# Four layers of a small transformer on one core: another passage from section to section

## The chip, the cores and the metric

The kernel runs on 1 core of one Trainium2 chip. The metric is the device time of one execution in microseconds (us), the median of several runs. Engines: TensorE (PE, and PEld for its weight loads), VectorE (DVE), ScalarE (ACT), GpSimd (POOL), and SyncE (SP), which issues the loads.

## The reference, cut to what matters

256 tokens of width 2048 pass through two layers with a mixer and an MLP each (`first_block`), and through two hybrid attention layers (`second_block`). Each of the six sections ends in the same way: a product with an output matrix, a norm over the features, an addition to the residual `h`; and the next section begins with a norm of the new `h`.

```python
def rmsnorm(x, g):
    y = x * lax.rsqrt(jnp.mean(x * x, axis=-1, keepdims=True) + RMS_EPS)
    return y * g

# first_block, per layer
mix = mixer(rmsnorm(h, norm_mix_pre[layer]), ...)          # ends in "@ w_out" or "@ w_o"
h = h + rmsnorm(mix, norm_mix_post[layer])
f = jnp.square(jax.nn.relu(rmsnorm(h, norm_mlp_pre[layer]) @ w_up)) @ w_down
h = h + rmsnorm(f, norm_mlp_post[layer])
# second_block, per layer
out = y @ w_out
x = x + rms_norm(out, post_w)
```

All of it is float32.

## The kernel before

**Layout.** Features lie on the partitions, tokens along the free axis: `h` is 16 blocks of 128 features x 256 tokens. All weight matrices are laid into one stream of chunks of 128 x 2048 values (1 MB). One chunk is one product: 16 units of 128 x 128, accumulated into one PSUM bank `acc[s]`, s = chunk number modulo 4.

**Float32 products from rounded parts.** Each chunk is split: ScalarE writes the rounded `w_high` (L719), VectorE the rest `w_low = raw - w_high` (L1119). Activations are split likewise (`x[:, kt, 0]` high, `x[:, kt, 1]` low). `high_unit` (L285) multiplies `w_high` with both activation parts side by side, 512 columns: the left half of the bank gets high x high, the right half high x low. `low_unit` (L292) adds `w_low` x high activations to the right half, 256 columns. Then ScalarE copies the right half to `corr` (L729), and VectorE adds the left half and `corr` (`sum_halves`, L1128). Both engines work three chunks ahead (`ahead`). The four `raw` buffers are loaded by SyncE, each load waiting for the product that used the buffer four chunks earlier (L251, L267 to L273).

**The passage.** In the output sections each block goes to `branch[b]`; after an MLP, VectorE adds it to the `branch[b]` of the earlier quarters (L1238). ScalarE squares the block (L735) and multiplies it by the norm's gain (`gain`, L754). GpSimd adds up the squares of blocks 0 to 14 (`add_squares`, L1077). After the last product `stat_post` on TensorE sums GpSimd's sum and the last square over the features (columns of ones, L354). VectorE's `mean` (L1139) divides, GpSimd's `root` (L1083) takes the power -0.5, VectorE writes two diagonal matrices from it (L1143), and TensorE multiplies them with ones (`spread`, L362), so that every partition of the bank `extra` has the scale of each token. `norm` on VectorE then goes through groups of one or two blocks (`NORM_GROUPS`): `step = branch * scale` (L1170), `h += step` (L1175), and `xs_low` (L1154), the low part of the next section's input; ScalarE writes the high part (L738) and the square of the new `h` (L735), and GpSimd adds these squares.

**The order.** Every engine's order is written out by hand, with counting semaphores between the engines; loops are hardware loops (`Fori`). TensorE starts the next section with `product_first`: chunks c, c+1 and c+2 together, block by block as `xs` becomes ready. Product c+3 follows, and has in its unit 0 (`STAT_AT`) the feature sums of the next norm and in unit 8 (`SPREAD_AT`) its spread. VectorE, in `norm`, does the subtraction of chunk c+2 between `mean` and the first step, that of c+3 behind the last `xs_low`, and then the mean and the copy of the scale to `scale_pre` (`norm_scale`, L1149), which the first results of the section need. There are five such passages, the sixth norm (c is None) is followed by the output's DMAs only. The two last layers are one loop of two turns, whose body on VectorE begins with `norm`'s part of the previous section and ends with `out_section`.

**Names used below.** r counts the norms' roots (24 in all), m the norms behind a section (0 to 5), n the norms ahead of one. PSUM banks `score[0]` and `score[1]` belong to the attention heads.

## Time and profile before

| | |
|---|---|
| median of 3 runs | 3194.34 us (3192.07 to 3197.99) |
| profiled execution: span, first to last instruction | 3191.0 us |
| instructions | 50316 |
| TensorE busy | 3054.0 us, 96% of the span |
| VectorE busy | 2115.3 us, 66% |
| ScalarE busy | 1591.5 us, 50% |
| GpSimd busy | 270.1 us, 8% |
| mean granted TensorE clock | 0.984 of full speed |
| DMA | 548.23 MB, mean 172 GB/s |

The profile is of one execution; its own time is the span and what lies around it (start and end of the program), and the runs' median is the number to compare. A row of a timeline has the start in us from the span's beginning, the duration in us, the engine, the line, the operation, `output<-inputs`, shapes, the count of merged instructions, and in brackets the idle time ahead of it and what ended it. Durations overlap slightly where instructions follow one another directly. A fp32 matmul appears as two records.

### The profile page before, as it was taken

The numbers are of one execution on the slowest core, as the hardware profiler recorded it, in microseconds if no ns is written. First come the engines' busy times: TensorE is split into PE (matmuls) and PEld (weight loads), VectorE is DVE, ScalarE is ACT, GpSimd is POOL, SyncE is SP. The second block draws the span as 40 slices with busy tenths as digits, with TensorE's granted clock in tenths as the row PEclk, the third lists the DMA queues.
The fourth block names the chain that finished last, engine by engine and source line by source line (L and its number), as shares of the span: only waits on it lengthen the run. The fifth ranks groups of instructions, "written<-read, shape, count | busy, mean of one in ns | idle before, by whom it ended". The sixth has DMA issues, their size and how long they took to land.

```text
span 3191.0 us, 50316 instructions
## 1 busy us (share of the span) xinstructions
PE 3054.0 (96%) x17552; PEld 2660.9 (83%) x17552; DVE 2115.3 (66%) x2969; ACT 1591.5 (50%) x2364; POOL 270.1 (8%) x206
## 2 busy tenths in 40 slices
PE   7999899999999899999999999999899998899997
PEld 6888788888888788887888888887788877788876
DVE  4776765756566677765756666665878655878655
ACT  5445544434444565555434444445657454657454
POOL 1002300000001300003000000003100003100003
PEclk9999999999999999999999999999999999999998
DMA  5555455555555344444555555554344434444434
GB/s 204 184 184 189 151 188 185 193 187 186 192 187 185 135 176 167 169 169 145 193 189 186 192 188 185 193 188 171 134 170 147 157 136 156 146 168 149 146 140 164
DMA packets 76413, 548.23 MB, mean 172 GB/s; under 512 B 8464, under 2 KB 8976, under 8 KB 10384
## 3 DMA queue, kind: packets, MB, share of 16 engines
q1 hardware_dynamic: 76304, 546.81, 47.7%
q8 instruction: 64, 1.05, 0.1%
q14 instruction: 45, 0.37, 0.0%
HBM read 544.68 MB, written 2.10 MB: 171 GB/s over the span
## 4 chain that ended last, share of the span: by engine, by line
PE 34%; issue 12%; POOL 3%; DVE 3%; ACT 1%; DMA 0%; POOLq 0%; DVEq 0%; ACTq 0%; SPq 0%
PE acc L285 20%; PE acc L292 10%; POOL sum_sq L1077 3%; PE acc L667 1%; PE score L385 1%; DVE w_low L1119 1%; DVE h L1175 0%; PE acc L674 0%; ACT w_high L719 0%; DVE step L1170 0%; PE head_out L412 0%; ACT swapped L818 0%; POOL small L1083 0%; PE score L393 0%; POOL sum_sq L1072 0%
## 5 line engine op out<-in xcount | busy, mean ns | idle before, releaser
L1119 DVE TENSOR_TENSOR w_low<-raw,w_high 128x2048 fp32r<-128x2048 f32 x514 | 1175.9, 2288 | 343.4 <-ACT w_high L719 343.0
L285 PE MATMUL acc<-xs,w_high 128*128 128x512 f32 x4962 | 1268.9, 400 | 50.3 <-DVE xs L1154 31.8
L285 PEld LDWEIGHTS acc<-xs,w_high 128*128 128x128 f32 x4962 | 921.2, 191 | 258.2 <-DVE xs L1154 39.0
L719 ACT ACTIVATE w_high<-raw 128x2048 fp32r<-128x2048 f32 x515 | 979.9, 1903 | 29.8 <-DMA raw<-stream 28.9
L729 ACT ACTIVATE corr<-acc 128x256 f32<-128x256 f32 x512 | 195.5, 382 | 1230.8 <-PE acc L292 1201.0
L285 PE MATMUL acc<-inner,w_high 128*128 128x512 f32 x3072 | 736.3, 391 | 2.8 <-DVE inner L1192 2.8
L292 PE MATMUL acc<-xs,w_low 128*128 128x256 f32 x4962 | 689.3, 285 | 0.9 <-DVE w_low L1119 0.9
L292 PEld LDWEIGHTS acc<-xs,w_low 128*128 128x128 f32 x4962 | 661.5, 194 | 25.1 <-DVE w_low L1119 1.4
L285 PEld LDWEIGHTS acc<-inner,w_high 128*128 128x128 f32 x3072 | 564.0, 188 | 112.6 <-DVE inner L1192 3.7
L1128 DVE TENSOR_TENSOR y<-acc,corr 128x256 f32<-128x256 f32 x408 | 172.3, 422 | 398.5 <-ACT corr L729 397.1
L292 PEld LDWEIGHTS acc<-inner,w_low 128*128 128x128 f32 x3072 | 393.7, 191 | 15.1
L292 PE MATMUL acc<-inner,w_low 128*128 128x256 f32 x3072 | 398.3, 283 | 0.0
L1077 POOL TENSOR_TENSOR sum_sq<-sum_sq,sq 128x256 f32<-128x256 f32 x162 | 230.3, 1421 | 285.7 <-ACT sq L735 278.8
L1072 POOL TENSOR_TENSOR sum_sq<-sq 128x256 f32<-128x256 f32 x12 | 21.0, 1754 | 1978.5 <-ACT sq L735 1960.8
L1128 DVE TENSOR_TENSOR branch<-acc,corr 128x256 f32 (+1 forms) x96 | 40.5, 422 | 121.4 <-ACT corr L729 121.4
L818 ACT ACTIVATE swapped<-y 32x256 f32<-32x256 f32 (+1 forms) x208 | 86.5, 416 | 42.0 <-DVE y L1128 39.1
L825 ACT ACTIVATE prob<-prob,small 128x128 f32<-128x128 f32 (+1 forms) x144 | 64.5, 449 | 70.7 <-DVE small L1276 41.3
L775 ACT ACTIVATE inner<-source 128x256 f32 (+1 forms) x176 | 71.7, 407 | 54.8 <-DVE source L1516 24.3
L1134 DVE TENSOR_TENSOR scaled<-y,scale_pre 128x256 f32<-128x256 f32 x208 | 88.4, 425 | 10.9
L738 ACT ACTIVATE xs<-h,col 128x256 fp32r<-128x256 f32 x96 | 46.8, 500 | 65.5 <-DVE h L1175 65.5
L1192 DVE TENSOR_TENSOR inner<-source,inner 128x256 f32 (+1 forms) x176 | 73.6, 418 | 1.9 <-ACT inner L775 1.9
L1083 POOL TENSOR_TENSOR small<-small,minus_half 128x2 f32<-128x2 f32 x24 | 16.7, 695 | 586.7 <-DVE small L1139 586.7
(141 smaller groups left out, 1339.1 us busy)
## 6 DMA issues: line engine op xcount, KB each, us to landing
raw<-stream SPq DMA_DIRECT2D x515, 1024.0 KB, 4.8
h<-x_t SPq DMA_DIRECT2D x4, 512.0 KB, 7.9
out<-h SPq DMA_DIRECT2D x4, 512.0 KB, 2.6
consts<-tables SPq DMA_DIRECT2D x1, 960.0 KB, 16.5
branch<-w_spatial SPq DMA_DIRECT2D x1, 512.0 KB, 17.3
branch<-b_spatial SPq DMA_DIRECT2D x1, 512.0 KB, 18.1
prob_t<-lambdas SPq DMA_DIRECT2D x1, 256.0 KB, 18.2
col<-columns SPq DMA_DIRECT2D x1, 136.0 KB, 2.1
```

The source lines that it names most:

```text
L285: nc.tensor.matmul(acc[s][:, :], w_high[:, s, kt * P:(kt + 1) * P], x[:, kt, :, :], start=(kt == first_of[0]), stop=False, skip_group_chec ...
L292: return nc.tensor.matmul(acc[s][:, TOKENS:], w_low[:, s, kt * P:(kt + 1) * P], x[:, kt, 0, :], start=False, stop=stop, skip_group_check=True)
L719: nc.scalar.activation(w_high[:, s, 0:units * P], raw[:, s, 0:units * P], ACT.Copy)\
L729: nc.scalar.activation(corr[:, s % 2, :], acc[s][:, TOKENS:], ACT.Copy).then_inc(corr_ready, 1)
L775: nc.scalar.activation(dyn2(inner, b, 0), source[:, s, :], ACT.Copy).then_inc(sem("inner_high"), 1)
L818: cp = nc.scalar.activation(swapped[a:a + half, :], src[b:b + half, :], ACT.Copy)
L825: nc.scalar.activation(prob[:, bank, lo:hi], prob[:, bank, lo:hi], ACT.Exp, bias=neg_max(bank, t), accum_out=denom(bank, t)).then_inc(sem( ...
L1077: nc.gpsimd.tensor_tensor(sum_sq[:, :], sum_sq[:, :], sq[:, b % 2, :], ALU.add)\
L1119: V.tensor_tensor(w_low[:, s, 0:units * P], raw[:, s, 0:units * P], w_high[:, s, 0:units * P], ALU.subtract).then_inc(low_ready, 1)
L1128: V.tensor_tensor(y[:, s % 2, :] if to is None else to, acc[s][:, 0:TOKENS], corr[:, s % 2, :], ALU.add)\
L1134: V.tensor_tensor(to, y[:, s % 2, :], scale, ALU.mult).then_inc(sem(done), 1)
L1192: V.tensor_tensor(dyn2(inner, b, 1), source[:, s, :], dyn2(inner, b, 0), ALU.subtract)\
```

## The change

1. The last product of the three output sections and of the two MLPs' last quarters (`product_last`, `last_products`) accumulates all three partial products into the left half of the bank: 32 matmuls of 256 columns with `w_high`, 16 with `w_low`. Between the two parts TensorE waits for GpSimd's fifteenth square sum and does its column sums. For this block `corr_out` and `sum_halves` go; ScalarE squares it from PSUM and writes `branch` with the gain in one activation (behind an MLP VectorE first adds it to `branch`). Small instructions keep the counters `corr_ready` and `summed` in step (`corr_skipped` on ScalarE, a copy of two columns to `unused` on VectorE).
2. `spread` has no diagonal: the root, broadcast along 128 columns, is the stationary operand and the identity the moving one, once for each half of the tokens. The two diagonal instructions and the buffer `diag` go, for all 24 roots.
3. In `norm` the product `branch * scale` is written to the PSUM banks `score[0]` and `score[1]` in turn instead of to `step`, and `h` is added from there; the wait of each multiply for the previous addition goes.
4. The subtraction (and the rounding) of chunk c+2 is done at the end of the output section, ahead of the mean, by the ordinary `ahead`.
5. `STAT_AT` goes from 0 to 4, `SPREAD_AT` from 8 to 12. `product_first` waits for one sum less. The sines and exponentials that ScalarE computed ahead of the first MLP come behind its first quarter. The last four blocks of the sections, and the last MLP quarter on TensorE, are written out behind the loops.

```diff
-STAT_AT, SPREAD_AT = 0, 8
+STAT_AT, SPREAD_AT = 4, 12
...
+            def product_last(c, s, x, m):
+                whole = acc[s][:, 0:TOKENS]
+                pe.wait_ge(high_ready, c + 1)
+                pe.wait_ge(summed, c - 3)
+                for kt in range(KB):
+                    for part in range(2):
+                        nc.tensor.matmul(whole, w_high[:, s, kt * P:(kt + 1) * P], x[:, kt, part, :],
+                                         start=(kt == 0 and part == 0), stop=False)
+                pe.wait_ge(sem("square_added"), squares_post(m) + KB - 1)
+                column_sums(sum_sq[:, :], True, False)
+                pe.wait_ge(low_ready, c + 1)
+                for kt in range(KB):
+                    mm = nc.tensor.matmul(whole, w_low[:, s, kt * P:(kt + 1) * P], x[:, kt, 0, :],
+                                          start=False, stop=(kt == KB - 1))
+                mm.then_inc(product_done, 1)
...
-                pe.wait_ge(summed, at(c))          # product_first
+                pe.wait_ge(summed, c - 1)
...
             def spread(r):
-                pe.wait_ge(sem("diag_ready"), r + 1)
-                nc.tensor.matmul(extra[:, 0:TOKENS], ones, diag[:, :], start=True, stop=True)\
-                    .then_inc(sem("spread_done"), 1)
+                pe.wait_ge(sem("root_ready"), r + 1)
+                for n in range(TB):
+                    mm = nc.tensor.matmul(extra[:, n * P:(n + 1) * P], root_of[:, n:n + 1].to_broadcast([P, P]), ident,
+                                          start=True, stop=True, skip_group_check=True)
+                mm.then_inc(sem("spread_done"), 1)
             def stat_post(m, r):
-                pe.wait_ge(sem("square_added"), squares_post(m) + KB - 1)
                 pe.wait_ge(sem("squared"), squares_post(m) + KB)
-                sum_over_features([sum_sq[:, :], sq[:, 1, :]], "square_added")
+                column_sums(sq[:, 1, :], False, True).then_inc(sem("square_added"), 1)
                 spread(r)
...
+            def corr_skipped(c):                   # ScalarE
+                act.wait_ge(summed, c - 1)
+                nc.scalar.activation(corr[:, 1, 0:TB], acc[3][:, 0:TB], ACT.Copy).then_inc(corr_ready, 1)
...
+                def last(b, s):                    # ScalarE, out_section
+                    ahead(c0 + b, s)
+                    square(acc[s][:, 0:TOKENS], squares_post(m) + b, s,
+                           lambda: act.wait_ge(product_done, c0 + b + 1))
+                    nc.scalar.activation(branch[:, b, :], acc[s][:, 0:TOKENS], ACT.Copy,
+                                         scale=column(G_POST + KB * m + b)).then_inc(sem("gained"), 1)
+                    corr_skipped(c0 + b)
...
             def root(r):                           # GpSimd
                 pool.wait_ge(sem("mean_ready"), r + 1)
+                pool.wait_ge(sem("spread_done"), at(r))
...
             def mean(r, count, eps, stat_sem, value):
                 dve.wait_ge(sem(stat_sem), value)
+                dve.wait_ge(sem("root_ready"), at(r))
                 V.tensor_scalar(mean_of, extra[:, TOKENS:TOKENS + TB], 1.0 / count, eps, ALU.mult, ALU.add)\
                     .then_inc(sem("mean_ready"), 1)
-                dve.wait_ge(sem("root_ready"), r + 1)
-                for n in range(TB):
-                    op = V.tensor_scalar(diag[:, n * P:(n + 1) * P], ident, root_of[:, n:n + 1], None, ALU.mult)
-                op.then_inc(sem("diag_ready"), 1)
...
                 mean(r, D, NORM_EPS, "square_added", squares_post(m) + KB)     # norm
-                if c is not None:
-                    low(c + 2, 2)
...
+                    stepped = score[i % 2][:, 0:width * TOKENS].rearrange("p (a t) -> p a t", a=width)
                     dve.wait_ge(sem("gained"), KB * m + b + width)
-                    dve.wait_ge(sem("h_ready"), at(KB * m + b))
-                    V.tensor_tensor(step[:, 0:width, :], branch[:, b:b + width, :], scale, ALU.mult)\
+                    V.tensor_tensor(stepped, branch[:, b:b + width, :], scale, ALU.mult)\
                         .then_inc(sem("step_ready"), width)
...
-                    V.tensor_tensor(h[:, b:b + width, :], h[:, b:b + width, :], step[:, 0:width, :], ALU.add)\
+                    V.tensor_tensor(h[:, b:b + width, :], h[:, b:b + width, :], stepped, ALU.add)\
                         .then_inc(sem("h_ready"), width)
...
+                if c is not None:
+                    dve.wait_ge(summed, c - 1)
+                    dve.wait_ge(corr_ready, c)
+                    V.tensor_copy(unused, acc[3][:, 0:TB]).then_inc(summed, 1)
                 for i in late:
                     xs_low(n, i)
...
+                        c = c0 + 2 * KB * q + 2 * KB - 1                      # VectorE, last MLP quarter
+                        ahead(c, 3)
+                        dve.wait_ge(product_done, c + 1)
+                        V.tensor_tensor(branch[:, KB - 1, :], branch[:, KB - 1, :], acc[3][:, 0:TOKENS], ALU.add)\
+                            .then_inc(sem("down_added"), 1)
```

## Rows read from the trace of the kernel before

**Rows 1.** The page: busy times, and the costliest ScalarE group (busy, mean ns).
```profile
PE 3054.0 (96%) x17552; PEld 2660.9 (83%) x17552; DVE 2115.3 (66%) x2969; ACT 1591.5 (50%) x2364; POOL 270.1 (8%) x206
...
L719 ACT ACTIVATE w_high<-raw 128x2048 fp32r<-128x2048 f32 x515 | 979.9, 1903 | 29.8 <-DMA raw<-stream 28.9
```

**Rows 2.** Timeline of PE, first passage: start, us, engine, line, operation, [idle before].
```profile
347.80 2.07 PE L292 MATMUL acc<-inner,w_low 128*128 128x256 f32 x16
...
351.89 0.59 PE L354 MATMUL extra<-consts,sq 128*128 128x1 f32 x4
354.02 1.22 PE L362 MATMUL extra<-diag,consts 128*128 128x256 f32 x2 [1.55 <-DVE diag L1143]
358.16 0.77 PE L285 MATMUL acc<-xs,w_high 128*128 128x512 f32 x1 [2.92 <-DVE xs L1154]
```

**Rows 3.** Timeline of VectorE, first passage.
```profile
352.51 0.16 DVE L1139 TENSOR_SCALAR small<-extra 128x2 f32<-128x2 f32 x1 [1.76 <-PE extra L354]
353.48 0.48 DVE L1143 TENSOR_SCALAR diag<-consts,small 128x128 f32<-128x128 f32 x2 [0.81 <-POOL small L1083]
353.88 2.28 DVE L1119 TENSOR_TENSOR w_low<-raw,w_high 128x2048 fp32r<-128x2048 f32 x1
356.08 0.41 DVE L1170 TENSOR_TENSOR step<-branch,extra 128x256 f32<-128x256 f32 x1
```

**Rows 4.** Windows, first passage: width, PE PEld DVE ACT POOL busy, clock, DMA.
```profile
354.00:356.00 2.00, 1.22 (x2) 0.50 (x2) 2.00 (x1) 0.00 (x0) 0.00 (x0) 0.50 0.06 25
358.16:381.74 23.58, 21.52 (x97) 16.75 (x97) 22.37 (x31) 15.24 (x35) 11.92 (x15) 0.88 0.00 1
```

**Rows 5.** Chain of waits: a product of 32 matmuls of 256 columns.
```profile
3031.17 3.84 PE acc L667 x32
```

**Rows 6.** Timeline of GpSimd, end of the last product.
```profile
346.91 2.54 POOL L1077 TENSOR_TENSOR sum_sq<-sum_sq,sq 128x256 f32<-128x256 f32 x1 [3.02 <-ACT sq L735]
```

**Rows 7.** Timeline of SyncE, and the page's row of the weight loads.
```profile
344.49 0.33 SPq L251 DMA_DIRECT2D raw<-stream  x1
...
raw<-stream SPq DMA_DIRECT2D x515, 1024.0 KB, 4.8
```

**Rows 8.** Timeline of VectorE, fifth passage, behind a jump back.
```profile
2698.69 0.16 DVE L1139 TENSOR_SCALAR small<-extra 128x2 f32<-128x2 f32 x1 [6.25 <-issue]
```

**Rows 9.** Timeline of VectorE, second passage, behind an MLP.
```profile
1082.88 0.16 DVE L1139 TENSOR_SCALAR small<-extra 128x2 f32<-128x2 f32 x1 [1.76 <-PE extra L354]
```

**Rows 10.** Timeline of VectorE inside the norm step, first passage.
```profile
359.48 1.22 DVE L1175 TENSOR_TENSOR h<-h,step 128x512 f32<-128x512 f32 x1
...
369.56 0.68 DVE L1170 TENSOR_TENSOR step<-branch,extra 128x512 f32<-128x512 f32 x1
370.16 1.03 DVE L1154 SCALAR_TENSOR_TENSOR xs<-h,col,xs 128x256 fp32r<-128x256 f32 x1
...
376.83 1.23 DVE L1175 TENSOR_TENSOR h<-h,step 128x512 f32<-128x512 f32 x1
```

**Rows 11.** Timeline of VectorE, the last norm step.
```profile
3177.59 0.69 DVE L1175 TENSOR_TENSOR h<-h,step 128x512 f32<-128x512 f32 x1
3178.41 0.69 DVE L1170 TENSOR_TENSOR step<-branch,extra 128x512 f32<-128x512 f32 x1
```

**Rows 12.** Timeline of GpSimd inside the norm step, first passage.
```profile
359.33 0.82 POOL L1072 TENSOR_TENSOR sum_sq<-sq 128x256 f32<-128x256 f32 x1 [5.88 <-issue]
```

**Rows 13.** Timeline of PE, end of the first three products and after.
```profile
381.74 0.50 PE L354 MATMUL extra<-consts,sum_sq 128*128 128x1 f32 x4
...
389.37 1.88 PE L285 MATMUL acc<-xs,w_high 128*128 128x512 f32 x7 [0.74 <-ACT w_high L719]
```

**Rows 14.** Timeline of VectorE, end of the norm step and the scale.
```profile
379.93 2.82 DVE L1119 TENSOR_TENSOR w_low<-raw,w_high 128x2048 fp32r<-128x2048 f32 x1
...
384.91 0.42 DVE L1149 COPY scale_pre<-extra 128x256 f32<-128x256 f32 x1 [0.79 <-PE extra L362]
```

**Rows 15.** Timeline of PE, a head's spread in the third layer.
```profile
2370.46 0.91 PE L362 MATMUL extra<-diag,consts 128*128 128x256 f32 x2 [2.54 <-DVE diag L1143]
```

More of the change, by code:

```diff
@@ L416, in weigh, with last_products, out_section, mlp_section @@
                 mm.then_inc(sem("head_done"), 1)
-            def out_section(c0, split0, late, order=None, hooks=None):
+            def last_products(c, m):
+                for s in range(3):
+                    product(c + s, s, inner)
+                product_last(c + 3, 3, inner, m)
+            def out_section(c0, split0, late, m, order=None, hooks=None):
                 product_early(c0, split0, late, order, hooks)
                 product(c0 + 3, 3, inner)
-                with pe.Fori(1, KB // 4) as i:
+                with pe.Fori(1, KB // 4 - 1) as i:
                     for s in range(4):
                         product(c0 + 4 * i + s, s, inner)
-            def mlp_section(c0, split0, n, r):
-                def quarter(q, first):
+                last_products(c0 + KB - 4, m)
+            def mlp_section(c0, split0, n, r, m):
+                def quarter(q, first, last):
                     c = c0 + 2 * KB * q
@@ L436, in quarter @@
                     product(c + 3, 3, inner)
-                    with pe.Fori(1, KB // 4) as i:
+                    with pe.Fori(1, KB // 4 - int(last)) as i:
                         for s in range(4):
                             product(c + 4 * i + s, s, inner)
-                quarter(0, True)
-                with pe.Fori(1, FFN_QUARTERS) as q:
-                    quarter(q, False)
+                    if last:
+                        last_products(c + KB - 4, m)
+                quarter(0, True, False)
+                with pe.Fori(1, FFN_QUARTERS - 1) as q:
+                    quarter(q, False, False)
+                quarter(FFN_QUARTERS - 1, False, True)
             product(0, 0, xs, ready=lambda kt: pe.wait_ge(sem("xs_ready"), kt + 1))
@@ L1195, in out_section, with one @@
             def out_section(c0):
-                def four(i, last):
-                    for s in range(4):
-                        c = c0 + 4 * i + s
-                        sum_halves(c, s, dyn(branch, 4 * i + s))
-                        if s < 3 or not last:
-                            ahead(c, s)
-                with dve.Fori(0, KB // 4 - 1) as i:
-                    four(i, False)
-                four(KB // 4 - 1, True)
+                def one(i, s):
+                    c = c0 + 4 * i + s
+                    sum_halves(c, s, dyn(branch, 4 * i + s))
+                    ahead(c, s)
+                with dve.Fori(0, KB // 4 - 1) as i:
+                    for s in range(4):
+                        one(i, s)
+                for s in range(3):
+                    one(KB // 4 - 1, s)
+                ahead(c0 + KB - 1, 3)
             def mlp_section(c0, split0, up0):
```

137 lines of the change are left out of this document (73 added, 64 removed).

## The prediction

> **What bounds the kernel.** I read the page first. TensorE is busy 96% of the span [rows 1], so only a time in which it waits can be won. In the long sections it does not wait; it waits where one section passes to the next. There are six such passages (five lead into three products computed together, the sixth is the last norm step), so I read the first in the timelines engine by engine, and laid the others beside it.
>
> The last product ends at 347.80 + 2.07 = 349.87, the next real matmul starts at 358.16: 8.29 us [rows 2]. The links: the ScalarE copy, the VectorE sum and the square of block 15 lie before the column sums that end at 352.48 [rows 2]; mean at 352.51, 0.81 for GpSimd's root, two diagonals of 0.48, then `w_low` of chunk 18 until 356.16, although the spread ended at 354.02 + 1.22 = 355.24 [rows 2, 3]. The step starts at 356.08, so the mean-to-step distance is 3.57, and 2.08 more pass to the first matmul.
>
> Behind it VectorE paces TensorE. From 358.16 to 381.74 VectorE is busy 22.37 of 23.58 us, TensorE idle 2.06, at a mean clock of 0.88 [rows 4]. That is (1 - 0.88) / 0.5 x 23.58 = 5.7 us at 1.2 GHz, the rest at 2.4; the clock had fallen while TensorE had only sums and the spread [rows 4].
>
> **The gap, behind a mixer (passages 1, 3, 5).** The last product becomes 32 + 16 narrow matmuls. The same form elsewhere takes 3.84 for 32 [rows 5], which is 0.12 each, so the high part lasts about what 16 wide ones last; I add 0.2. Between the parts TensorE now waits for GpSimd's add of block 14, which ends at 346.91 + 2.54 = 349.45, since a VectorE subtraction runs at the same time [rows 6]. So 1.5 us of stall, 0.5 for four column sums (0.59 with the pipeline end [rows 2]) and 2.07 for the low part: the product ends near 352.1, 2.2 later. In return the corr copy and the VectorE sum go, and the square starts at once: 352.1 + 0.45, sums 0.59, mean possible at 353.3.
>
> But the moved subtraction has its own chain. Load issued 344.49, landed 4.8 later [rows 7] at 349.3; `w_high` 1.90 [rows 1] to 351.2; `w_low` 2.28 [rows 3] to 353.5. It stands ahead of the mean on VectorE, so the mean starts at 353.45, 0.94 later than now. Root and spread follow as before, without the diagonals (0.03 + 0.48), and without the 0.85 by which `w_low` outlasted the spread: mean to step 3.57 - 0.51 - 0.80 = 2.26. Step at 355.7: **0.35 earlier**. If the load landed a microsecond later this turns to a loss of 0.65; if GpSimd alone decided, the gain would be 0.5. The new waits queue the square, the gain and the small skip copy behind `w_high` on ScalarE; it would have been done 0.9 before the product ends, so nothing is late by it. For the spread, two 128-column products take the place of one of 256: I take the same 1.22; ends: 0.3 shorter (a spread in the third layer takes 0.91 [rows 15]) and 0.6 longer (four records of sums take 0.59).
>
> Passage 5 has a jump back of the layer loop ahead of the mean: 6.25 us of idle without a releaser [rows 8]. The jump is now reached behind `w_low`'s dispatch, about 0.9 later. Same balance: 0.35 earlier.
>
> **Behind an MLP (passages 2, 4).** Here VectorE must still add the last product to `branch`, and that add stands behind `w_low`. In the first passage `w_low` ends 1.0 behind the old mean; here the old mean of 1082.88 [rows 9] already has that add ahead of it, so `w_low` ends 0.5 behind it, at 1083.4. Add 0.41 [rows 3], hop and square 0.55, hop and sums 0.7: mean at 1085.1, 2.2 later; minus 1.31: step **0.9 later**. Bounds: 0 (load earlier) to 2 later. Sum of the five gaps: 3 x -0.35 + 2 x 0.9 = +0.7 us.
>
> **The norm step.** `h` += `step` on 512 columns takes 1.22 to 1.23 nearly everywhere in the five passages, while the sixth, where GpSimd adds no squares, shows 0.69 [rows 10, 11]. In the passage GpSimd's add started at 359.33 and ended at 360.15; `h` started at 359.48 and ended at 360.70, 0.55 behind it [rows 10, 12]: one waits until the other is through. The multiply, which reads `branch` and PSUM, takes 0.68 beside GpSimd [rows 10]. So two SBUF inputs collide and one does not, and with the step in PSUM `h` has one. I take 0.68 for it. A result written to PSUM by VectorE is in no row; lower bound 0.68, upper bound 1.22, the slowest row of the form; I take 0.68, the row with a PSUM operand.
>
> The Trainium skill (VectorE: DVE Perf Modes, the TRN2 errata) charges a PSUM source 62 cycles more than an SBUF one, about 65 ns. By it 54 adds would cost 3.5 us more. The multiply with its PSUM source at 0.68 beside an SBUF-only add at 0.69 speaks against it [rows 10, 11], and the sum below goes by the rows.
>
> Period of a pair of blocks now: 359.48 to 376.83 is six periods, 2.89 each [rows 10]. New: 0.60 multiply (369.56 to 370.16 [rows 10]) + 0.60 add + two `xs_low` of 0.4 (what other work on 256 columns takes, 0.41 [rows 3]) = 2.0, if nothing collides. But `xs_low` has two SBUF inputs, and GpSimd's two adds (0.82 each [rows 12]) still come in each period; the one that collides takes 1.03 [rows 10]. One of two colliding gives 2.6. Five periods save 5 x 0.4 = 2.0; the first saves 0.5 and its multiply no longer waits for the previous add (0.2 twice); the last add 0.55; back go 0.5 where ScalarE's `w_high` in the middle now makes VectorE wait. VectorE is through 3.0 earlier (bounds: 1.0 at the old period, 4.5 at 2.0).
>
> TensorE's floor: 48 pairs of wide and narrow matmuls at 0.12 x 3 = 0.36 [rows 5] are 17.3, plus half of 5.7 cold: 20.1 against 23.58. It can win 3.5 at most; I take 3.0 with VectorE. Then product 4: it waits 0.74 for `w_high`, which comes behind the scale [rows 13], so the scale decides. Now it stands at 384.91, 3.17 behind the end at 381.74 [rows 13, 14]. The spread moves to unit 12: 12 x 0.24 = 2.9, the sums at unit 4 another 0.36, the spread itself 0.79 (the idle time before the copy [rows 14]): 4.05 behind that end, although its input is ready earlier (the diagonals' 0.5 are gone). So 0.9 go back, and of 3.0 remain **2.1 per passage**, 10.5 in five (bounds 1.5 x 5, where VectorE stays the later and saves 1.0 + 0.5, and 3.5 x 5).
>
> **The tail.** Mean 0.9 later, minus 0.5 for the diagonals: +0.4. The multiply no longer waits for the previous add: now 3178.28 to 3178.41 [rows 11], 0.13, and back-to-back instructions overlap by 0.08 (369.56 + 0.68 against 370.16 [rows 10]): 0.21 x 8 = 1.7. Sum -1.3.
>
> **The rest.** Without the diagonal the spreads of the heads come 0.5 earlier; TensorE waits 2.54 for one, and there is one such in each of two layers [rows 15]. Together -1.0 (0 to -2). The first norm and the latent ones lie beside other work. The sines and exponentials that move behind the first MLP quarter fall where ScalarE, busy 50% of the span [rows 1], is three chunks ahead of TensorE: nothing. Without that cover, its 1.90 for one `w_high` is the size of what a product could wait.
>
> **Sum.** +0.7 - 10.5 - 1.3 - 1.0 = -12.1 us on the profiled span of 3191.0. The median of the runs is 3194.34, 3.3 above that span (launch and end around it, unchanged), so 3182.2; I say 3182.
>
> **Rivals.**
> 1. *TensorE becomes the bound.* `xs_low` hardly collides, the period is 2.0 to 2.2 and each passage wins 3.5; gaps as good as zero: 3194.3 - 17.5 - 2.5 (tail and heads) = 3174. For it: the adds that collided most were `h`. Against: GpSimd's work in the passage stays the same. 15%.
> 2. *The gain is eaten at new seams.* New code is laid straight behind loops; if two more seams pay what the fifth does (6.25 of idle where others have 1.76 [rows 3, 8]: 4.5 each), 9 go back: 3191. The same comes out if collisions move to both `xs_low` and the gaps grow 1 us each. Within 0.2%. 20%.
> 3. *Slower: VectorE from PSUM to PSUM.* If multiply and add each take 1.22, the period is 3.2 before collisions, 3.6 with them, 0.7 above now. Seven pairs at 0.7 are 4 to 5 in each passage, 1.08 more for each of seven pairs less 1.7 are 6 in the tail: 3194 + 20 + 6 = 3220. It turns to a loss once both together cost 0.8 more than I take. For it: no row shows a VectorE result in PSUM. Against: reads of PSUM cost nothing extra here. 8%.
> 4. *Slower by the moved subtraction alone:* the chain load, `w_high`, `w_low`, mean runs 3 us longer in every passage because ScalarE takes it late: +15 against -12: 3197. 4%.
>
> My forecast has 53%. Under 0.2% (6.4 us, about what a measurement of this kernel can tell) counts as the same. Faster: 53 + 15 + a few of rival 2, 71%; same 18%; slower 11%. Range 3168 to 3194: down to rival 1 with all bounds good, up to rival 2's end.
>
> **What would show it.** Right: `h` at 0.68 to 0.70 in the passages; `xs_low` still at times near 1.0; a hole of 1.5 us inside each last product; mean later by 0.9 (mixer) and 2.2 (MLP); first three products done in 20.5 us instead of 23.6; a product 4 that still waits for `w_high`. Wrong: a multiply above 0.75, a period above 2.8, idle time without releaser at new seams, or a mean that is not later.

## The result, and the profile after

The changed kernel takes 3167.93 us (median of 4 runs, 3166.22 to 3171.5) against 3193.2 beside it (3191.23 to 3197.99): ratio 0.9917, 95% interval 0.9904 to 0.9929. It is 25 us faster, twice the 12 predicted, and its median lies just outside the range of 3168 to 3194.

The last product in the first passage, TensorE (start, us, ..., [idle before]), against [rows 2]:

```profile
345.75 4.00 PE L318 MATMUL acc<-inner,w_high 128*128 128x256 f32 x32
351.09 0.61 PE L368 MATMUL extra<-consts,sum_sq 128*128 128x1 f32 x4 [1.34 <-POOL sum_sq L1126]
351.56 2.15 PE L324 MATMUL acc<-inner,w_low 128*128 128x256 f32 x16
354.18 0.61 PE L368 MATMUL extra<-consts,sq 128*128 128x1 f32 x4 [0.47 <-ACT sq L766]
355.97 0.71 PE L379 MATMUL extra<-consts,small 128*128 128x128 f32 x4 [1.18 <-POOL small L1133]
358.81 0.77 PE L284 MATMUL acc<-xs,w_high 128*128 128x512 f32 x1 [2.13 <-DVE xs L1201]
```

VectorE beside it, against [rows 3]:

```profile
352.77 2.29 DVE L1169 TENSOR_TENSOR w_low<-raw,w_high 128x2048 fp32r<-128x2048 f32 x1 [2.32 <-ACT w_high L745]
354.98 0.15 DVE L1190 TENSOR_SCALAR small<-extra 128x2 f32<-128x2 f32 x1
356.72 0.43 DVE L1215 TENSOR_TENSOR score<-branch,extra 128x256 f32<-128x256 f32 x1 [1.58 <-PE extra L379]
```

The hole inside the product is there (1.34 us), and `w_low` ends as the mean starts. Counted from the start of the last product, the mean comes 9.23 later where it came 8.36 later (352.51 - 344.15), and the step follows it by 1.74, where it was 3.57.

VectorE in the norm step, against [rows 10], and GpSimd beside it, against [rows 12]:

```profile
363.62 0.68 DVE L1220 TENSOR_TENSOR h<-h,score 128x512 f32<-128x512 f32 x1
364.21 0.48 DVE L1201 SCALAR_TENSOR_TENSOR xs<-h,col,xs 128x256 fp32r<-128x256 f32 x1
364.61 0.69 DVE L1215 TENSOR_TENSOR score<-branch,extra 128x512 f32<-128x512 f32 x1
365.21 0.48 DVE L1201 SCALAR_TENSOR_TENSOR xs<-h,col,xs 128x256 fp32r<-128x256 f32 x1
365.61 0.68 DVE L1220 TENSOR_TENSOR h<-h,score 128x512 f32<-128x512 f32 x1
...
374.01 1.58 DVE L1201 SCALAR_TENSOR_TENSOR xs<-h,col,xs 128x256 fp32r<-128x256 f32 x2
```
```profile
361.58 6.70 POOL L1126 TENSOR_TENSOR sum_sq<-sum_sq,sq 128x256 f32<-128x256 f32 x7 [0.87 <-ACT sq L766]
...
363.45 0.85 POOL L1126 TENSOR_TENSOR sum_sq<-sum_sq,sq 128x256 f32<-128x256 f32 x1
```

`h` fell from 1.22 to 0.68. Of the 80 `xs_low` of the five passages 72 take 0.47 to 0.50. The other eight, 0.67 to 0.88, are the last one or two of each passage, where no instruction of 512 columns with a PSUM operand lies between one `xs_low` and the next (the row at 374.01 merges two of them, 0.69 and 0.87). In the kernel before 35 of 80 were longer than 0.5.

Two blocks take 1.99. That is the undisturbed period; over the same six periods as in the 2.89 of the kernel before, which hold one wait for ScalarE in either kernel, it is 2.13 ((372.76 - 359.97) / 6). GpSimd's seven additions begin 0.99 apart; the first takes 0.73, the others 0.85. Over the five passages its 75 additions take 0.82 on average, where they took 0.81: the time that VectorE no longer loses is not lost by GpSimd instead.

The first three products, against [rows 4] (width, busy time of PE, PEld, DVE, ACT, POOL, granted clock), and in the second line the low part of the last product of the second passage:

```profile
358.81:377.70 18.89, 18.89 (x96) 16.54 (x97) 17.66 (x32) 13.55 (x32) 12.19 (x15) 0.87 0.00 1
1077.00:1080.00 3.00, 3.00 (x15) 2.74 (x13) 2.12 (x1) 0.85 (x1) 0.00 (x0) 0.50 0.00 0
```

They take 18.89 us, not 23.58, and TensorE is never idle in them. Product 4 and the product behind it, against [rows 13, 14]; the third row is the same place in the third passage:

```profile
380.95 0.61 PE L379 MATMUL extra<-consts,small 128*128 128x128 f32 x4
...
386.05 3.93 PE L284 MATMUL acc<-xs,w_high 128*128 128x512 f32 x16 [1.68 <-ACT w_high L745]
...
1519.81 5.53 PE L284 MATMUL acc<-xs,w_high 128*128 128x512 f32 x16 [2.56 <-ACT w_high L745]
```

The wait for `w_high` grew from 0.74 to 1.68, and where it is 2.56 the sixteen matmuls behind it run partly at 1.2 GHz (5.53 for 3.93).

The mean and the copy of the scale cut the whole span into pieces. That is the account used from here on (profiled executions; us):

| kernel | up to first mean | five times mean to scale | five times scale to next mean | last mean to end | span |
|---|---|---|---|---|---|
| before | 352.5 | 162.7 | 2656.9 | 19.0 | 3191.0 |
| changed | 355.0 | 135.6 | 2662.4 | 16.7 | 3169.7 |
| e1 | 354.1 | 139.0 | 2656.1 | 17.3 | 3166.5 |
| e3 | 354.2 | 138.7 | 2672.0 | 17.0 | 3181.9 |
| e4 | 352.9 | 143.4 | 2641.7 | 16.2 | 3154.2 |
| e5 | 354.5 | 132.1 | 2662.3 | 16.7 | 3165.7 |
| e9 | 353.3 | 138.3 | 2659.9 | 16.7 | 3168.2 |
| e11 | 351.8 | 138.3 | 2642.9 | 16.3 | 3149.2 |
| e14 | 351.6 | 137.3 | 2649.2 | 16.3 | 3154.4 |

The change takes 27.1 out of the passages and 2.2 out of the tail, and puts 8.0 (2.5 + 5.5) on the rest. Of the 8.0, 5.8 lie between the start of the last product and the mean: the mean comes 0.87, 2.07, 0.89 and 2.10 later in the first four passages, 2.33 earlier in the fifth and 2.16 later in the sixth. The fifth mean, and the low part of the sixth last product, which ran mostly at 1.2 GHz (3.26 for 2.15):

```profile
2685.60 0.16 DVE L1190 TENSOR_SCALAR small<-extra 128x2 f32<-128x2 f32 x1 [1.14 <-PE extra L368]
3148.19 3.26 PE L324 MATMUL acc<-inner,w_low 128*128 128x256 f32 x16
```

The other 2.2 lie in the sections. Two cautions go with the table. The profiled execution is not the median one: in the changed kernel and e3 it was 3.6 and 2.6 slower than the median, in e4 and e11 2.9 and 6.9 faster. And before and e1, which have the same instructions up to the first mean, differ by 1.6 there. So much can differ in the first and the third column without a cause in the code.

### The profile page after: what moved, and what is told of

Read it like the earlier page. It is cut to its first block, busy times and chain, and to the rows that moved or that the text cites. A ratio compares the mean times of both kernels' runs of the same rounds, so it can differ in the third digit from the quotient of the medians.

```text
span 3169.7 us, 50419 instructions
## 1 busy us (share of the span) xinstructions
PE 3049.9 (96%) x17696; PEld 2676.1 (84%) x17696; DVE 2078.0 (66%) x2921; ACT 1590.9 (50%) x2364; POOL 304.8 (10%) x206
## 4 chain that ended last, share of the span: by engine, by line
PE 41%; issue 5%; DVE 3%; ACT 2%; POOL 1%; DMA 1%; DVEq 0%; POOLq 0%; ACTq 0%; SPq 0%
PE acc L284 24%; PE acc L291 12%; POOL sum_sq L1126 1%; PE score L402 1%; DMA raw<-stream 1%; PE acc L693 1%; ACT w_high L745 1%; DVE w_low L1169 1%; PE acc L700 0%; ACT swapped L866 0%; DVE prob L1323 0%; DVE small L1327 0%; PE extra L379 0%; PE head_out L429 0%; PE score L410 0%
## 5 line engine op out<-in xcount | busy, mean ns | idle before, releaser
L284 PE MATMUL acc<-inner,w_high 128*128 128x512 f32 x2976 | 713.5, 392 | 2.8 <-DVE inner L1241 2.8
L284 PEld LDWEIGHTS acc<-inner,w_high 128*128 128x128 f32 x2976 | 546.8, 188 | 108.8 <-DVE inner L1241 3.7
L291 PEld LDWEIGHTS acc<-inner,w_low 128*128 128x128 f32 x2976 | 381.5, 191 | 14.5
L291 PE MATMUL acc<-inner,w_low 128*128 128x256 f32 x2976 | 386.0, 283 | 0.0
L1126 POOL TENSOR_TENSOR sum_sq<-sum_sq,sq 128x256 f32<-128x256 f32 x162 | 265.2, 1637 | 228.1 <-ACT sq L766 217.7
L1184 DVE TENSOR_TENSOR scaled<-y,scale_pre 128x256 f32<-128x256 f32 x208 | 88.4, 425 | 10.9
L1133 POOL TENSOR_TENSOR small<-small,minus_half 128x2 f32<-128x2 f32 x24 | 16.7, 695 | 596.0 <-DVE small L1190 596.0
```

Of the source, the lines that this page charges most:

```text
L284: nc.tensor.matmul(acc[s][:, :], w_high[:, s, kt * P:(kt + 1) * P], x[:, kt, :, :], start=(kt == first_of[0]), stop=False, skip_group_chec ...
L291: return nc.tensor.matmul(acc[s][:, TOKENS:], w_low[:, s, kt * P:(kt + 1) * P], x[:, kt, 0, :], start=False, stop=stop, skip_group_check=True)
L1126: nc.gpsimd.tensor_tensor(sum_sq[:, :], sum_sq[:, :], sq[:, b % 2, :], ALU.add)\
L1184: V.tensor_tensor(to, y[:, s % 2, :], scale, ALU.mult).then_inc(sem(done), 1)
```

## The experiments

### Which part brings the gain

**e1**, the kernel before with part 3 alone.
```diff
-dve.wait_ge(sem("h_ready"), at(KB * m + b))
-V.tensor_tensor(step[:, 0:width, :], branch[...], scale, ALU.mult)
+V.tensor_tensor(stepped, branch[...], scale, ALU.mult)    # stepped lies in score[g % 2]
```


> The kernel before, with the norm step in PSUM alone (part 3 of the change). Theory A (slots): the addition to h no longer needs both SBUF inputs, GpSimd's adds fit into the 0.6 us slots between two xs_low, so xs_low stays at 0.48 and a pair of blocks takes 2.0 us instead of 2.9; the scale then comes 4 to 5 us earlier in each of five passages, 1.7 us in the tail: 3193 - 20 to 25, about 3171, or some 8 us more if TensorE's clock falls at product 4. Theory B (my forecast: one of two xs_low collides, period 2.5 to 2.6): 2.7 per passage and 1.7, about 3178. Theory C (the gain comes mainly from other parts): above 3185.

Measured: 3169.45 us (3168.21 to 3171.01), ratio 0.9934 (0.9917 to 0.995). That is theory A's time to 2 us, and its durations:

```profile
364.20 0.48 DVE L1154 SCALAR_TENSOR_TENSOR xs<-h,col,xs 128x256 fp32r<-128x256 f32 x1
364.60 0.68 DVE L1175 TENSOR_TENSOR h<-h,score 128x512 f32<-128x512 f32 x1
```

**e2**, the changed kernel with the step back in SBUF: e1's edit undone.

> The changed kernel with the step in SBUF again (part 3 undone). Theory A: additions at 1.22 us beside GpSimd's adds, period 2.9, each passage 3.5 to 4.5 us longer, the tail 1.7: 3168 + 17 to 24, about 3188. Theory C: under +6, below 3174.

Measured: 3196.72 us (3191.41 to 3198.5), ratio 1.0012 (1.0002 to 1.0021). `h` is back at 1.22:

```profile
364.36 1.22 DVE L1221 TENSOR_TENSOR h<-h,step 128x512 f32<-128x512 f32 x1
```

Parts 1, 2, 4 and 5 together bring nothing. Part 3 is the gain. (Not each of the other parts is worth nothing: e4 and e9 below show that one of them costs what the others bring.)

**e3**, the changed kernel with the diagonals (part 2 undone).

> The changed kernel with the two diagonal instructions and the one wide spread (part 2 undone). Theory: 0.5 us for the diagonals and 0.5 us for the wide spread at the low clock in each of six gaps, 0.5 in each of two heads' waits; the scale of the next section hides the rest behind the hook: +6 to +8 us, about 3175. Rival (diagonals lie beside other work, as I priced them but for the tail): +3, 3171.

Measured: 3181.05 us (3177.32 to 3183.97), 13 above the changed kernel. By the table 3.1 of the profile's 12.2 lie in the passages, where the two diagonal instructions (0.48 together [rows 3]) can account for 2.4; 9.6 lie in the sections, whose instructions are the same but for the diagonals of the heads. The mean granted clock was 0.980, against 0.984.

**e10**, the kernel before with parts 3 and 2.

> The kernel before with part 3 (the product of the norm step in PSUM) and part 2 (no diagonal), and nothing else. Part 3 alone gave 3169.5. Theory A (the diagonals are worth what their instructions last on the path: nothing in a passage, where the subtraction behind them fills the time, 0.5 in the tail, 1 to 2 at the heads): 3166 to 3168. Theory B (they are worth what putting them back cost in the changed kernel, 13 us, most of it where TensorE's shorter idle time keeps the granted clock up): 3157 to 3161.

Measured: 3168.95 us, as e1; theory B's 3157 to 3161 is not seen. But its five executions go from 3163.06 to 3180.94, and their clocks with them, from 0.984 to 0.977: 0.007 of 3170 us is 22, the times differ by 18. One kernel, with nothing changed, is so moved by its clock as far as e3 was moved from the changed kernel. Beside e1 the diagonals are worth nothing that this scatter lets one see. That they are worth a few us, what their instructions last, is not shown; the rest of e3's 13 is no property of part 2 that these runs show, though e3's five clocks (0.980 to 0.983) all lie at or below the changed kernel's lowest (0.983).

### Who waited for whom

**e7**, the kernel before, GpSimd adding 2 of 256 columns (sums of the next norm left out but for two tokens).
```diff
-nc.gpsimd.tensor_tensor(sum_sq[:, :], sum_sq[:, :], sq[:, b % 2, :], ALU.add)
+nc.gpsimd.tensor_tensor(sum_sq[:, 0:2], sum_sq[:, 0:2], sq[:, b % 2, 0:2], ALU.add)
```


> The kernel before, with GpSimd's additions of squares ahead of a norm on 2 of 256 columns (leaves out the sum of squares of all tokens but two in five norms; the work of all other engines is the same). Theory A (all that the passage paid in the kernel before is that VectorE and GpSimd wait for one another at SBUF): the additions to h fall to 0.69, xs_low to 0.48, the period of a pair from 2.9 to 2.1 us, product_first from 23.6 to about 19.5, and the kernel to 3170 to 3175. Theory B (the step in SBUF is itself slower, also without GpSimd): h stays at 1.22 in the passages and the time within 5 us of 3193.

Measured: 3173.6 us (3172.19 to 3174.63), ratio 0.9939 (0.9923 to 0.9955). VectorE:

```profile
362.90 0.67 DVE L1171 TENSOR_TENSOR step<-branch,extra 128x512 f32<-128x512 f32 x1
363.50 0.48 DVE L1155 SCALAR_TENSOR_TENSOR xs<-h,col,xs 128x256 fp32r<-128x256 f32 x1
363.91 0.68 DVE L1176 TENSOR_TENSOR h<-h,step 128x512 f32<-128x512 f32 x1
```

With the step in SBUF, but GpSimd nearly quiet, `h` is 0.68 and the period 2.0. Theory A: the 1.22 was GpSimd's doing. The Trainium skill (GPSIMD Engine Reference, Specifications) says that GpSimd contends for SBUF with VectorE instructions that have two SBUF inputs; the runs agree, 1.22 against 0.68, and give it its size.

**e8**, the same cut in the changed kernel.

> The changed kernel with the same cut of GpSimd's additions to 2 columns (leaves out the same sums). Theory A (with the step in PSUM nothing is left of the contention on the path): the period stays at 2.0, xs_low at 0.48, 3165 to 3169; only what GpSimd's last additions delay the sums may be won. Theory B (GpSimd still slows VectorE by half of what it did): the period falls below 1.9 us and the kernel to 3160 or less.

Measured: 3167.17 us (3165.19 to 3169.02), 0.8 below the changed kernel. On VectorE only the eight long `xs_low` at the ends of the passages became shorter (none is above 0.50), and mean to scale takes 135.6 in five passages, as in the changed kernel. Theory A: nothing of the contention is left to win.

**e6**, the changed kernel with sixteen groups of one block.
```diff
-NORM_GROUPS = [(0, 1), (1, 1)] + [(b, 2) for b in range(2, KB, 2)]
+NORM_GROUPS = [(b, 1) for b in range(KB)]
```


> The changed kernel with the norm step in sixteen groups of one block instead of two single ones and seven pairs. An addition of one block from PSUM takes about 0.41 us, so GpSimd, if it only gets at SBUF while VectorE reads PSUM or is idle, finds slots of 0.4 instead of 0.6 us. Theory A (GpSimd's adds go into the slots of VectorE's PSUM instructions, and they need the long ones): the xs_low collide again at 0.7 to 1.0 us, the period of two blocks goes from 2.0 to 2.8 or more, five passages of seven periods lose 25 us or more: 3190 or more. Theory B (with one PSUM operand in the addition there is no collision whatever the length): xs_low stays at 0.48, only the fixed part of fourteen more instructions in each passage is added, about 0.05 to 0.15 us each: 3172 to 3178.

Measured: 3197.56 us, ratio 1.0014 (1.0005 to 1.0024).

```profile
361.61 0.42 DVE L1215 TENSOR_TENSOR score<-branch,extra 128x256 f32<-128x256 f32 x1
362.27 0.48 DVE L1201 SCALAR_TENSOR_TENSOR xs<-h,col,xs 128x256 fp32r<-128x256 f32 x1 [0.24 <-ACT xs L769]
362.67 0.41 DVE L1220 TENSOR_TENSOR h<-h,score 128x256 f32<-128x256 f32 x1
```

Theory A had the time and the period (2.78), but not the reason: `xs_low` stays at 0.48 as theory B had it, and GpSimd's additions take 0.73 to 0.83. What costs is 0.24 of wait for ScalarE in front of each `xs_low`, which with one block lies right behind its `h`, and two more fixed parts for each pair. So pairs serve two ends: few instructions, and time for ScalarE.

### The end of the last product

**e4**, the changed kernel with the subtraction of chunk c+2 behind the mean, and all column sums behind the last product.
```diff
-        ahead(c0 + KB - 1, 3)              # end of the output section
...
         mean(r, D, NORM_EPS, "square_added", squares_post(m) + KB)
+        low(c + 2, 2)
```


> The changed kernel with the rounding of chunk c+2 behind the last square and its subtraction behind the mean (part 4 undone), and with the column sums of GpSimd's total behind the last product instead of inside it. Theory (the moved subtraction sets the step behind an MLP, where the last addition to branch stands behind it): behind an MLP the mean comes 3 us earlier and the step 1.6 earlier, behind a mixer 0.5 earlier: 3168 - 5 = 3163. Rival (the moved subtraction is the gain that I missed): slower than 3168 by 3 or more.

Measured: 3158.86 us (3155.97 to 3161.91), ratio 0.9902 (0.9885 to 0.9919), faster than both kernels. The second passage, TensorE and then VectorE of the first:

```profile
1070.01 4.00 PE L318 MATMUL acc<-inner,w_high 128*128 128x256 f32 x32
1073.85 2.08 PE L322 MATMUL acc<-inner,w_low 128*128 128x256 f32 x16
1076.89 0.61 PE L368 MATMUL extra<-consts,sq 128*128 128x1 f32 x4 [0.62 <-ACT sq L766]
```
```profile
352.89 0.16 DVE L1190 TENSOR_SCALAR small<-extra 128x2 f32<-128x2 f32 x1 [2.33 <-PE extra L368]
354.03 2.29 DVE L1169 TENSOR_TENSOR w_low<-raw,w_high 128x2048 fp32r<-128x2048 f32 x1 [0.97 <-ACT w_high L745]
356.24 0.42 DVE L1217 TENSOR_TENSOR score<-branch,extra 128x256 f32<-128x256 f32 x1
```

From the start of the last product the mean comes after 7.0 us (mixer; changed kernel 9.2) and 7.5 (MLP; 10.9), the step after 10.4 and 10.9 (11.0 and 12.6). The subtraction lies in the time in which root and spread are awaited anyway. In the table e4 gives back 7.8 between mean and scale, and wins 22.8 against the changed kernel in the first and third columns. Of these 14.4 lie between the start of the last product and the mean (2.2 behind a mixer, 3.2 to 3.6 behind an MLP and in the sixth, nothing in the fifth, where the jump shows again: 3.30 of idle without a releaser ahead of TensorE's last sums); for the other 8.4 no cause in the code is known. Against e1, timed beside it, e4 is 10.6 faster: with the subtraction where the kernel before had it, the rest of the change does bring something.

**e9**, the changed kernel with only the column sums moved behind the product.

> The changed kernel with one edit: TensorE takes the column sums of GpSimd's fifteen squares behind the low part of the last product, not between its parts. The subtraction of chunk c+2 stays ahead of the mean. Theory A (the subtraction decides when the mean comes, the hole inside the product hardly matters: VectorE ended it at 355.06, 0.1 before the mean, in the first passage): means at most 0.5 us earlier in six passages and one cold stretch less, 3164 to 3168. Theory B (the hole of 1.34 us and the cold low part behind it are what the last product pays): 1.3 us per passage and a cold low part less in three or four, 3156 to 3160, as good as the kernel with the subtraction behind the mean as well (3159).

Measured: 3172.71 us (3169.95 to 3174.38), ratio 0.9938 (0.9921 to 0.9955), 14 above e4 and 5 above the changed kernel. TensorE of the second passage, VectorE of the first:

```profile
1073.91 2.08 PE L322 MATMUL acc<-inner,w_low 128*128 128x256 f32 x16
1075.83 0.50 PE L368 MATMUL extra<-consts,sum_sq 128*128 128x1 f32 x4
1080.22 0.81 PE L368 MATMUL extra<-consts,sq 128*128 128x1 f32 x4 [3.89 <-ACT sq L766]
```
```profile
351.05 2.29 DVE L1169 TENSOR_TENSOR w_low<-raw,w_high 128x2048 fp32r<-128x2048 f32 x1 [2.31 <-ACT w_high L745]
353.26 0.15 DVE L1190 TENSOR_SCALAR small<-extra 128x2 f32<-128x2 f32 x1
```

The product is through 1.3 earlier, and the mean comes at the same distance, 9.23 (353.26 - 344.03): the hole was hidden behind the load, `w_high`, `w_low` chain. e4 differs from it by the places of the subtraction and of the rounding that feeds it. Against e4 it pays 18.6 in the first and third columns (15.2 of it between last product and mean) and wins 5.1 in the second. In the first passage the mean comes 3.31 behind the product's end, in e4 1.11: 0.9 of the 2.2 is the rounding, which ScalarE does ahead of the last square, and 1.3 the subtraction, which VectorE does ahead of the mean. Theory B falls. Theory A had the cause but no loss; what goes with the loss is that TensorE's idle time is now in one piece, and the spread behind it takes 1.22 in all five passages, instead of 0.71 in four.

### The scale, the rounding and the clock

**e5**, the changed kernel with `STAT_AT, SPREAD_AT = 0, 8`.

> The changed kernel with the next norm's sums and spread back at units 0 and 8 of product 4 instead of 4 and 12. Theory A (the spread sets the scale, the scale lets ScalarE through to the rounding that product 4's successors wait for, and a long idle of TensorE there costs twice because the granted clock falls behind it): spread and scale 0.9 us earlier in each passage, the idle of 1.7 to 3.3 us ahead of the next product 0.5 to 0.9 shorter, 3 to 7 us in all: 3161 to 3165. Theory B (GpSimd's adds or the xs_low decide when the scale is ready, the hooks are not what is late): within 2 us of the changed kernel's 3168.

Measured: 3168.56 us (3167.47 to 3169.98), no change. In the table 3.5 are won in the passages; the profile's span is 4.0 shorter, the medians are not (e5's profile is of its fastest execution, the changed kernel's of its slowest). The mean clock of its executions is 0.9816, that of the changed kernel's 0.9838. By time theory B; the wait ahead of the next product did shrink to 0.74, as A had it.

**e11**, e4 with the same two numbers.

> The changed kernel with the subtraction of chunk c+2 behind the mean and the sums behind the last product (3158.9 when timed before), and now also the next norm's sums and spread at units 0 and 8. In the changed kernel itself the units gave nothing in the whole (3168.6), though product 4's wait shrank. Theory A (the scale comes about 1.4 us earlier in each passage as it did there, and it stays won where the clock does not fall): 3152 to 3156. Theory B (what the scale wins is lost again before the next loads land): 3157 to 3161.

Measured: 3157.76 us (3150.91 to 3162.02), ratio 0.9894 (0.9877 to 0.991). The best of all, but not told apart from e4.

**e12**, e11 with ScalarE's `w_high` of chunk c+4 ahead of the split and the swaps.
```diff
-                            if not (first_four and s == 0):
+                            if first_four and s == 0:
+                                ahead(c + 1, 1)
+                            elif not (first_four and s == 1):
                                 ahead(c, s)
                             split_high(src0 + KB * q + j, j, s % 2)
```


> As the kernel before this one, and ScalarE rounds the weights of chunk c+4 ahead of the small instructions that wait for the scale (the split, the swaps), so that the product behind product 4 does not wait for them. Theory A (product 4's successor waits for w_high, 0.74 to 3.3 us in each of five passages, because the rounding stands behind what the scale releases): all of these waits go, 3 to 8 us: 3147 to 3153. Theory B (the rounding waits for its load, issued only when product c is done, not for the scale): the waits stay and the split comes later by 1.9 us: 3154 to 3162.

Measured: 3160.66 us (3159.66 to 3165.34). ScalarE in the first and the third passage:

```profile
382.99 1.91 ACT L745 ACTIVATE w_high<-raw 128x2048 fp32r<-128x2048 f32 x1 [4.57 <-DMA raw<-stream]
...
1516.16 1.91 ACT L745 ACTIVATE w_high<-raw 128x2048 fp32r<-128x2048 f32 x1 [6.99 <-DMA raw<-stream]
```

In the first passage the wait of the next product went (0.74 in e11), in the third it grew from 0.79 to 2.27. Theory B's time, and its reason: the rounding waits for its load (4.57 and 6.99), which the product four chunks earlier releases. Once the scale is no longer late, the load is.

**e13** and **e14** fill TensorE's gap: the changed kernel with four matmuls ahead of the spread and eight behind it, and e11 with four and fourteen.
```diff
+            def keep_busy(count):
+                for _ in range(count):
+                    nc.tensor.matmul(head_out[:, 0:P], ident, ident, start=True, stop=True, skip_group_check=True)
...
                 column_sums(sq[:, 1, :], False, True).then_inc(sem("square_added"), 1)
+                keep_busy(4)
                 spread(r)
+                keep_busy(14)
```


> The changed kernel with twelve more matmuls of 128 columns on TensorE in each gap, into a bank that nobody reads: four ahead of the spread, where it waits 1.0 to 1.2 us for the root, and eight behind it, where it waits 2.1 us for the first xs. One takes about 0.18 us at full clock and 0.36 at half. Theory A (the clock falls behind a gap because TensorE stood idle in it; about 2.5 of the 18.9 us of the first three products go that way): the first three products run at full clock, the share lost to the clock falls from 51 us by 8 to 12, and the kernel takes 3156 to 3161. Theory B (the clock falls in the gap for another reason, or what the matmuls put in its place is too little): the loss stays at 50, and the eight matmuls, at half clock 2.9 us long, hold the first product back by up to 0.8 in each passage: 3168 to 3172.

> The kernel with the subtraction behind the mean, the sums behind the last product and the units 0 and 8 (3157.8 when timed), with the same matmuls: four ahead of the spread and fourteen behind it, where TensorE waits 3.7 us. Theory A (idle time is what lowers the clock): the loss falls from 49 us to 38 to 41, the time to 3146 to 3150. Theory B (it is not, or the matmuls collide with something): 3157 to 3163, the upper end if fourteen at half clock, 5.0 us, outlast the gap.

Measured: e13 3167.95 us (3163.85 to 3169.92), e14 3157.92 us (3156.1 to 3162.68): both as without the filling. (The kernel before took 3197.4 beside these two and 3193 beside the changed kernel and e11. By the ratios, 0.9906 against 0.9917 and 0.9884 against 0.9894, 3 us may have been won; their intervals overlap, so it is not shown.) Yet the clock did what theory A said: the mean over the executions rose from 0.9838 to 0.9888 and from 0.9845 to 0.9898. e11's first three products in the first passage, and then e14's:

```profile
357.22:376.10 18.88, 18.88 (x100) 16.36 (x100) 17.66 (x32) 13.56 (x32) 12.18 (x15) 0.90 0.00 1
```
```profile
357.06:376.00 18.94, 17.99 (x101) 15.12 (x101) 17.72 (x32) 13.57 (x32) 12.20 (x15) 1.00 0.00 1
```

At 0.90 TensorE is busy 18.88 of 18.88 us, at 1.00 it is busy 17.99 of 18.94, and the stretch is no shorter. Here a TensorE without idle time was not the bound: a slow clock had stretched its matmuls to the pace of VectorE's `xs_low`. The third passage, where e11's clock was lower, is different (e11, then e14):

```profile
1484.80:1504.22 19.42, 19.42 (x96) 16.95 (x97) 18.20 (x32) 13.55 (x32) 12.18 (x15) 0.85 0.00 1
```
```profile
1484.96:1503.58 18.62, 17.83 (x96) 14.76 (x97) 17.40 (x32) 13.56 (x32) 12.18 (x15) 1.00 0.00 1
```

At 0.85 the slow clock cost 0.8. Likewise e13 takes 1.8 less than the changed kernel from step to scale, in the five passages together. But it loses 1.3 of that again ahead of the step: in two of its passages the added matmuls themselves ran at 1.2 GHz and held back the spread behind them (in the second the step follows the mean by 2.77 instead of 1.74). From mean to scale 0.5 (e13) and 1.0 (e14, against e11) are left. So theory A holds for the clock and falls as to the time; theory B has the time, not the reason: what the clock stretches was for the most part paced by VectorE.

## Why the prediction was right or wrong

Sum of the predicted terms against the profiled execution:

| term | predicted | measured |
|---|---|---|
| mean later: 4 x 0.94 + 2 x 2.2 behind the products, heads -1.0 | +7.2 | +8.0 |
| mean to first step, five times | -6.6 | -8.3 |
| first step to scale, five times | -10.5 | -18.8 |
| last mean to end | -2.2 | -2.2 |
| together | -12.1 | -21.3 |

**Right.** The last product's chain in the first four passages: the mean 0.87 later behind the mixer (predicted 0.94) and 2.07 behind the MLP (2.2: from 1082.88 - 1074.06 = 8.82 to 1081.65 - 1070.76 = 10.89), decided by `w_low` as said, e9 showing it. The tail from the mean on, to 0.1. `h` at 0.68 and the multiply at 0.69 with a result in PSUM. (The multiply that I read as one beside GpSimd, at 369.56, had no addition beside it; the one at 363.86 had, from 363.98 to 364.72, and took 0.67. The reading stands.) No surcharge on a PSUM source, which the Trainium skill (VectorE: DVE Perf Modes, the TRN2 errata) would have asked for: the same `h` takes 0.68 from PSUM and 0.68 from SBUF (e7).

**Luck: the first row of the table.** In the fifth passage I had the mean 0.9 later; it is 2.33 earlier, because the jump, which I carried over whole, is hidden. In the sixth I had 0.9 and it is 2.16, with the low part at the low clock. Together the six give +5.8 where I had +8.2. The sections, where I had -1.0 for the heads, give +2.2. That the sums come out at 7.2 and 8.0 proves none of the terms.

**Wrong: "one of two `xs_low` collides", the period of 2.6.** This is the term that failed: -10.5 predicted from step to scale, -18.8 measured. I kept GpSimd's work as a sum that has to land on VectorE somewhere. But between two `xs_low` there is now, except at the end of a passage, always an instruction with a PSUM operand, 0.60 from start to start. GpSimd's addition goes on there and takes 0.85, against 0.74 at its shortest. The period is 1.99, and the subtraction behind the last `xs_low` starts 18.80 behind the first step instead of 23.85: 5.05 earlier where I had 3.0. The sum was also added up wrongly: from 2.89 to 2.6 in five periods is 1.45, not 2.0, which makes 2.4 of the 3.0; and the upper bound of 4.5 is the five periods at 2.0 alone, with the other terms of the same sum 5.4.

**Wrong: TensorE's floor of 20.1.** I took 0.36 a pair of matmuls plus half of all the time lost to the low clock before. The loss was smaller (0.13 x 18.89 = 2.5 against 2.8), and a pair takes 0.35 at full clock (in e14 they start at 374.51 and 374.86). The stretch took 18.89, and even that was nearly VectorE's pace. Rival 1, "TensorE becomes the bound" with 3.5 a passage at 3174, was nearer than the forecast in its period and its size. Its bound is one in part only: at full clock TensorE has 0.95 to spare (e14), at the clock granted in the changed kernel (0.86 to 0.87) it costs some tenths of a microsecond in a passage (e13 against it, 1.8 in five).

**Wrong in size: the spread at 1.22.** It took 0.71 in four of five passages. The 1.22 of [rows 2] was its time at 1.2 GHz ([rows 4]: granted clock 0.50). That part 1 keeps the clock up, by keeping TensorE at work until shortly before, is not shown: e9, whose idle time is in one piece, has 1.22 five times, but e11, with the sums at the same place, has 0.71 three times. The step follows the mean by 1.74 in three passages, 2.26 was predicted.

**Right in direction, not settled in size: the later hooks.** I charged 0.9 a passage; e5 wins 0.7 a passage in the profile, and nothing in the medians.

**Rivals 2 to 4.** No seam costs time in the changed kernel: the jump of the fifth passage is hidden behind `w_low`, and the mean there waits 1.14 where it waited 6.25 [rows 8]. No PSUM-to-PSUM cost. The moved subtraction doesn't make the kernel slower than before, but it is the part that should not have been made: e4 against e9 puts 14 us on it, with its rounding.

**A small one.** The 3.3 between the span and the median are not all launch and end: an execution is 1.7 to 1.8 longer than its span (3171.5 and 3169.7), the rest is that the profiled one was faster than the median.

**What stays open.** Why e3 and e5 run at a lower mean clock than the changed kernel, and where the 2.2 in the sections come from. e10 shows that executions of one kernel differ by as much, so differences of 5 to 10 us between these kernels carry that caution; the account by stage, where it finds the same number in each passage, does not.

## What to carry to other kernels

Where two engines slow one another at SBUF, put one operand of the long instruction into PSUM and see which of the two waits then: here it was worth as much as making the other engine's work vanish (e1 and e7). A piece of work belongs into a wait that stays (here root and spread), not ahead of it, even if its input is ready early. And an engine busy all the time need not be the bound: raise its clock or fill its gaps once, and see in each place whether the stretch gets shorter.

## What the runs showed of the hardware that was not expected

- GpSimd's addition of 256 columns takes 0.73 to 1.00 in the passages of the kernel before, 0.81 on average, and 0.73 to 0.86 in the changed one, 0.82 on average. VectorE's instructions of 512 columns with a PSUM operand took 0.67 to 0.69 whatever GpSimd did, those with both inputs in SBUF up to 1.24 for 0.68 and, with 256 columns, up to 1.03 for 0.48. The 2048-column subtraction beside GpSimd takes 2.83 for 2.29.
- The granted clock fell to 0.50 inside a product, behind a hole of 1.34 us ahead of which TensorE had worked without a break (second passage, 1077 to 1080), and not in the first passage behind the same hole. With twelve to eighteen matmuls without use in the gap the first three products ran at 0.99 to 1.00 in all five passages, against 0.86 to 0.87 in the changed kernel; in two passages of each the gap itself was at 0.50 for at least a part.
- Executions of one kernel differed by up to 18 us with the mean granted clock (e10).
